# Mixing stage of a hybrid encoder step: the transposes of tiles 1 and 2 moved to other places in TensorE's order

## What is computed

```python
def _rms_norm(x, g):
    xf = x.astype(jnp.float32)
    y = xf * lax.rsqrt(jnp.mean(xf * xf, axis=-1, keepdims=True) + RMS_EPS)
    return (y * g.astype(jnp.float32)).astype(x.dtype)
...
    # end of _diff_attention, per head of 128 values
    o = o * lax.rsqrt(jnp.mean(o * o, axis=-1, keepdims=True) + RMS_EPS)
    o = o * subln_g.astype(jnp.float32) * (1.0 - lam_init)
...
    mixed = jnp.concatenate([od, osb], axis=-1)      # 512 + 512 columns
    hp = xp + mixed @ w_out[l]                       # 1024 x 1024
    xp = hp + _swiglu(hp, norm_ffn_g[l], w_gate[l], w_up[l], w_down[l])
```

## Time and profile before

| what | us |
| --- | --- |
| median of 3 runs | 1412.73 |
| lowest and highest of the 3 | 1412.57, 1413.26 |
| the profiled execution's own time | 1409.75 |
| its span, first to last instruction | 1407.9 |
| TensorE busy in it | 1361.4 |
| VectorE busy in it | 999.7 |
| mean granted TensorE clock | 0.993 of full speed |

### The profile page before, as it was taken

One profiled execution on the slowest core, in us unless ns is written; L12 is line 12 of the kernel. 1 busy time (PEld: TensorE's weight loads), 2 busy tenths in 40 slices (PEclk: granted clock), 3 DMA queues, 4 the chain that ended last, 5 costly groups with the idle time before them and its releaser, 6 DMA issues. The chain is left out here.

```text
span 1407.9 us, 23796 instructions
## 1 busy us (share of the span) xinstructions
PE 1361.4 (97%) x9152; PEld 1193.8 (85%) x9152; DVE 999.7 (71%) x1317; ACT 623.8 (44%) x1112; POOL 450.8 (32%) x416
## 2 busy tenths in 40 slices
PE   6999999989999999999789999999999999999997
PEld 5778888768888777788689999999999998787886
DVE  5896858688868999756687766566766566754466
ACT  6634333288887887333352122222132233533343
POOL 2133341200010000111174454454454454644353
PEclk9999999999999999999999999999999999999999
DMA  7265542464444544433234543444443448855554
GB/s 254 72 213 192 204 154 73 146 181 138 126 127 121 148 136 135 156 127 96 65 121 144 174 137 123 150 145 145 174 143 116 150 163 290 303 175 164 164 180 172
DMA packets 172200, 218.05 MB, mean 155 GB/s; under 512 B 19836, under 2 KB 110328, under 8 KB 170680
## 3 DMA queue, kind: packets, MB, share of 16 engines
q1 hardware_dynamic: 163416, 193.13, 42.3%
q0 software_dynamic: 3840, 12.58, 2.7%
q10 hardware_dynamic: 4832, 10.82, 2.1%
HBM read 152.98 MB, written 63.50 MB: 154 GB/s over the span
## 5 line engine op out<-in xcount | busy, mean ns | idle before, releaser
L792 PE MATMUL ps_proj<-shared 128*128 128x512 f32 x224 | 90.1, 402 | 2.7 <-DVE shared L546 1.8
L2663 ACT COPY aux<-ps_feed 128x544 f32<-128x544 f32 x22 | 13.5, 612 | 170.3 <-PE ps_feed L2984 170.3
L793 PE MATMUL ps_proj<-shared 128*128 128x512 f32 x224 | 88.1, 393 | 0.0
L794 PE MATMUL ps_proj<-shared 128*128 128x512 f32 x224 | 88.1, 393 | 0.0
L2613 POOL TENSOR_TENSOR ring_more<-staging,ring_more 128x512 fp32r<-128x512 f32 x45 | 69.5, 1550 | 56.5 <-ACT ring_more L2649 56.4
L2613 POOL TENSOR_TENSOR shared<-staging,shared 128x512 fp32r<-128x512 f32 x41 | 60.0, 1467 | 86.1 <-ACT shared L2649 86.1
L1431 ACT COPY aT<-ps_aT 128x512 f32<-128x512 f32 (+2 forms) x168 | 81.1, 526 | 9.8 <-PE ps_aT L1760 9.0
L1760 PE MATMUL ps_aT<-ident,z 128*128 128x128 f32 (+1 forms) x568 | 83.3, 280 | 1.9 <-DVE z L1603 1.7
L2877 DVE TENSOR_TENSOR blocks<-ps_feed,blocks 128x512 f32<-128x512 f32 x56 | 36.0, 682 | 66.4 <-PE ps_feed L3013 66.4
L1603 DVE TENSOR_TENSOR_SCAN z<-z,near 128x1024 f32<-128x1024 f32 (+7 forms) x64 | 81.5, 1336 | 0.0
L2982 PE MATMUL ps_feed<-shared,ring_more 128*128 128x272 f32 x264 | 76.6, 290 | 2.4 <-issue 2.4
(11 more groups left out here) (372 smaller groups left out, 4520.5 us busy)
## 6 DMA issues: line engine op xcount, KB each, us to landing
staging<-s_dram SPq DMA_DIRECT2D x50, 256.0 KB, 4.2
staging<-in_w_gate SPq DMA_DIRECT2D x11, 1024.0 KB, 7.8
blocks<-in_w_up SPq DMA_DIRECT2D x11, 1024.0 KB, 5.3
blocks<-in_w_down SPq DMA_DIRECT2D x11, 1024.0 KB, 9.8
t_dram<-blocks SPq DMA_DIRECT2D x11, 1024.0 KB, 3.9
s_dram<-blocks SPq DMA_DIRECT2D x11, 1024.0 KB, 5.2
w_raw<-in_w_in SPq DMA_DIRECT2D x10, 1024.0 KB, 6.6
staging<-in_cache_sb_v POOLq DMA_DIRECT2D x31, 256.0 KB, 3.1
```

The source lines that it names most:

```text
L792: nc.tensor.matmul(res, a_hi[:, k, cols], b_hi[:, k], start=start, stop=False)
L793: nc.tensor.matmul(res, a_hi[:, k, cols], b_lo[:, k], start=False, stop=False)
L794: return nc.tensor.matmul(res, a_lo[:, k, cols], b_hi[:, k], start=False, stop=(k == HK - 1))
L2663: nc.scalar.copy(two(first), bank(u, 0)).then_inc(first_done, 1)
```

## The change

Two of the nine calls of `turn_m` move in TensorE's program; nothing is added or removed, and the programs of the other engines stay as they were. `turn_m(1)` moves from between the two left-half products of tile 0 to ahead of the wait for the left half of tile 0. `turn_m(2)` moves from ahead of the products of tile 1 to between its two output halves, just ahead of `turn_n(0)`.

```diff
             multiply_first(0, range(HK, KD))
             turn_m(0)
             multiply_first(1, range(HK, KD))
+            turn_m(1)
             pe.wait_ge(m_lo, 2)
             multiply_first(0, range(HK)).then_inc(mixed, 1)
-            turn_m(1)
             multiply_first(1, range(HK)).then_inc(mixed, 1)
             pe.wait_ge(*t["outputs_made"])
             for i in range(1, NT):
                 n = tiles[i][1]
-                if i + 1 < NT:
+                if 2 < i + 1 < NT:
                     turn_m(i + 1)
                 pe.wait_ge(m_lo, 2 * (i + 1))
                 for j in range(2):
...
                     last.then_inc(mixed, 1)
+                    if j == 0 and i == 1:
+                        turn_m(2)
                     if j == 0:
                         turn_n(i - 1)
```

## The result

| | before | changed |
| --- | --- | --- |
| median of 22 runs, us | 1412.74 | 1414.4 |
| lowest to highest | 1410.71 to 1415.44 | 1413.19 to 1421.37 |
| the profiled execution's own time | 1409.75 | 1415.26 |
| its span | 1407.9 | 1413.5 |
| mean granted clock | 0.993 | 0.990 |

The ratio of the times is 1.0017, with a 95% interval of 1.0011 to 1.0023: the change makes the kernel 2.4 us slower (1.6 to 3.2). The medians of the table differ by only 1.66 us; both figures lie in the interval, so the size of the loss is known to about 1 us and not better. The two profiled executions are 5.5 us apart, far more than that.

What follows compares the result with a forecast made beforehand. TensorE, busy 97% of the span, was taken to bound the kernel, so only its idle stretches matter. Moved wait +1.39 and clock net +1.0 gave +2.4 us, 1415.1 us; range 1412.8 to 1417.6.

Steps and rivals of the forecast that it cites:

- the free turn: Turn of tile 1, 12 matmuls sooner: its data are ready, no wait is added, same 0.35 us; cost 0.
- the moved wait: Ahead of `turn_n(0)`: the 2.52 us idle before tile 2's turn goes, 3.92 idle opens here; 1.39 us later.
- The price of the clock behind the new gap: After the new gap, TensorE at half pace: 1.46 us lost, bounds 0 to 2.45.
- What before pays: At the old 2.52 us gap, some timed executions of before lose the clock too: a third, 0.5.
- The net of the two: Clock price behind the new gap less what before pays at its old gap: net +1.0 us.
- the clock holds: Rival: in the new gap the clock stays up as in the old one; +1.4, 1414.1 us; chance 0.17.
- Falls early and comes back late: Rival, middle of tile 1: 2.45 lost instead of 1.0; +3.9, 1416.6 us, up to +4.9; chance 0.21.
- The rival by which the gain stays: Held cast does not hold up `norm(0)`; `turn_n(0)` at 594.74, -2.8, 1409.9 us; gain or nothing 0.05.
- the clock at the end of the stage: Later gap at 692 to 700: if shifted, full speed may return after up to 4.9 us, 1.0 more, +4.9.

Runs made afterwards that it cites:

- turn 1 alone: Against the kernel before, only the turn of tile 1 is moved earlier; the turn of tile 2 stays ahead of the products of tile 1: 1.0003.
- turn 2 alone: Against the kernel before, only the turn of tile 2 is moved later, between the output halves of tile 1: 1.0023.
- The filled gap: The changed kernel with 16 thrown-away matmuls between the turn of tile 2 and `turn_n(0)`: 1.0004 against before.
- Turn 2 after 12 matmuls: The changed kernel with the turn of tile 2 after 12, not all 24, matmuls of tile 1's left columns: 0.9980 against before.
- norm behind right half: The changed kernel with `turn_n(0)` moved behind the right half of tile 1: 0.9980 against before.
- Both in the middle: The changed kernel with the turn of tile 2 after 12 matmuls of tile 1's left columns and `turn_n(0)` after 12 of the right: 0.9966 against before.
- Before filled: The kernel before with 9 thrown-away matmuls in its old gap, ahead of the turn of tile 2: 0.9989.
- squares and norm first: The changed kernel with tile 0's squares ahead of tile 2's cast on ACT and its norm ahead of the low part on DVE: 0.9963 against before.

## Why the prediction was right

The forecast was +2.4 us and the ratio gives +2.4. Two large parts of it, the free turn and the moved wait, were right each by itself. The two parts on the clock were both too small and largely cancelled, as one is subtracted from the other. That the sums agree to a tenth is luck: the second comparison of the same two kernels gave +1.8 (0.4 to 3.3).

1. **The turn of tile 1 is free.** Right. With turn 1 alone, 1.0003. The prediction feared that the early load of tile 3 crowds that of tile 2. No such effect shows: in the eight traces with the early turn, DVE began on tile 2 between 7.58 and 8.16 us after the turn of tile 0. In before it was 7.90, and in the kernel with turn 2 alone, where the load of tile 3 is not early, 8.27.
2. **The wait moves to `turn_n(0)` and grows.** Forecast +1.39, idle 3.92; the trace has +1.42 and 3.96. The chain is confirmed link by link: cast 0.64 us behind the turn, squares 0.48 behind the cast, norm 2.10 behind the squares, line 2133 0.06 behind the norm. The experiment with the squares first shows that ACT's and DVE's order causes it.
3. **The price of the clock behind the new gap: mis-sized.** I took 1.46, by the row of 2.9 us at half pace behind the gap at the end of the stage. Three traces have 2.55 to 2.85, all beyond the upper bound of 2.45. The clock was low for as long here (599.2 to 606.0) as at either place of the prediction (290.3 to 297.1, 696.5 to 703.3), 6.8 us. What counts is how much of that is work. Here it was 5.85 us. At the end of the stage a second wait of 2.20 us stood in the middle of it, and I took only the 2.9 us behind that wait. The 5.85 us give the price: eight transposes that take 0.83 us longer, and 4.23 us of products at one per 0.427 us in place of 0.234, which is 1.91; together 2.74, for 2.75 in the trace.
4. **What before pays: mis-sized the same way.** I gave a third of 1.46, 0.5. Two of three traces that have this wait at its old place lost 1.5, and filling the gap gained 1.6 (0.3 to 3.0), so it probably pays in most executions; the interval would also allow one in five.
5. **The net of the two** was forecast at 1.0; from the traces it is about 2.7 less 1.0 to 1.5, so 1.2 to 1.7. Added to 1.42 that is 2.6 to 3.1, within the interval of 1.6 to 3.2. The sum came out closer than its parts deserve.

A check of this account over all kernels: take before with its clock lost (26.09 us to turn 3) as the typical execution and subtract. The changed kernel gives +2.6, timed 2.4, and in its repeat +2.4, timed 1.8. Turn 1 alone -0.3, timed +0.4. Turn 2 alone +2.7, timed 3.3. The filled gap -0.1, timed +0.6. Turn 2 after 12 matmuls and norm behind right half -2.7, each timed -2.8. Both in the middle -4.2, timed -4.8. Before filled -1.6, timed -1.6. Only squares and norm first falls out: -3.3, timed -5.2 (-6.9 to -3.5). Its trace shows nothing for the rest within the stage. A part can lie ahead of it, where no kernel differs: the first product of the stage starts anywhere from 575.66 us (in this very trace) to 579.67 in the twelve traces. Whether that is all of it stays open. The same spread is why one profile cannot stand for the time. Of the 5.6 us between the first two spans, 1.18 lie ahead of the turn of tile 0, 4.17 between it and turn 3 (28.72 less 24.55), and 0.25 behind.

The rivals: "the clock holds" is out, in three traces of three. "Falls early and comes back late" describes the trace (1.2 GHz until 606.0, 5.9 us of work) and priced it best, with 2.45; that it did not end at its +3.9 is because before pays as well. The rival by which the gain stays needed ACT's order changed, and with that order changed it came.

The rival "falls early and comes back late" had one more term, up to 1.0 us for the clock at the end of the stage. The traces settle it. The changed kernel did have the longer slow stretch there: the clock fell at 701.6 and was back only at 711.8, against 696.5 to 703.3 in before. But by the next wait of TensorE it had cost nothing. The first two lines here are of before, the other two of the changed kernel:

```profile
700.36 0.57 PE L2982 MATMUL ps_feed<-parts_early,shared 128*128 128x272 f32 x1 [2.20 <-PEq L3169]
712.61 0.36 PE L2982 MATMUL ps_feed<-shared,ring_more 128*128 128x272 f32 x1 [1.63 <-issue]
...
705.70 0.57 PE L2984 MATMUL ps_feed<-parts_early,shared 128*128 128x272 f32 x1 [2.20 <-PEq L3171]
717.94 0.36 PE L2984 MATMUL ps_feed<-shared,ring_more 128*128 128x272 f32 x1 [0.24 <-issue]
```

From the first of each pair to the second are 12.25 and 12.24 us, and 12.23 to 12.25 in all twelve traces. TensorE waits at the second line in every one, and slower work only shortens this wait, here from 1.63 to 0.24. So the row from which the 1.46 was taken did not lose that time either: a slow clock costs only where TensorE's own work sets the pace.

The rule cited from the Trainium skill ("TensorE: Matmul & The Clock Gate", section "HAM oscillation — how this bites in real kernels"), that a long wait between bursts makes the next one start cold, holds here: cold at 600.15 behind 3.96 us. The same page (section "What's actually happening") has the moment of a transition vary from run to run. The kernel before shows more than that: behind one wait of 2.52 us the clock fell in one execution and not in another.

## What to carry to other kernels

Before moving work on one engine to fill its wait, look at what every in-order engine behind it has queued after the instruction that waits for it: here one cast on ACT stood between a turn that nobody needed yet and a norm that TensorE needed next. Two cures worked: the turn at the earliest place at which its data were ready, in the middle of a run of matmuls (0.9980, and 0.9966 with the norm's turn moved too), or the late turn kept and the other engines' programs put in the order in which their results are needed (0.9963). And a wait on TensorE costs more than its length if the clock falls with it: count how much work falls into the slow stretch and whether anything waits for that work, and ask of the kernel before whether it pays too, since one profile may be the lucky one.

## What was not expected of the hardware

- The clock can fall after the gap is over. In the kernel before, with a wait of 2.52 us it fell at 593.0, with transposes and matmuls running again since 592.54, and came back at 596.4.
- Work that is thrown away can make a kernel faster: nine matmuls in the gap of before, 2.1 us of TensorE time at 0.234 each, gained 1.6 us (0.3 to 3.0).
- Eight transposes at 1.2 GHz took from 600.15 to 601.77, 1.62 us, against 0.79 at 2.4 GHz, 2.05 times as long. The products went from one per 0.234 us to one per 0.427, 1.8 times.
- A slow clock need not cost time. Behind the stage's last wait it was at 0.50 for 2.9 us of work in before and for 6.1 in the changed kernel, and the next wait of TensorE ended 12.25 and 12.24 us after that work began.
